# The time-mix scan: mask by block level taken from the solved products to the known triangular factor

## The reference

```
def step(S, inp):
    r_t, w_t, k_t, v_t, a_t, b_t = inp
    sa = jnp.einsum('bhij,bhj->bhi', S, a_t)
    S = S * w_t[:, :, None, :] + sa[..., None] * b_t[:, :, None, :] + v_t[..., None] * k_t[:, :, None, :]
    return S, jnp.einsum('bhij,bhj->bhi', S, r_t)
```

## Time and profile before

| | us |
|---|---|
| three runs: median (lowest to highest) | 1450.24 (1449.11 to 1451.15) |
| the profiled execution, its own time | 1440.16 |
| its span in the trace | 1438.4 |
| TensorE busy | 1405.0 (98%) |
| DVE busy | 926.4 (64%) |
| ACT busy | 326.8 (23%) |
| GpSimd busy | 26.6 (2%) |

### The profile page before, as it was taken

One profiled execution on the slowest core, in us unless ns is written; L12 is line 12 of the kernel. 1 busy time (PEld: TensorE's weight loads), 2 busy tenths in 40 slices (PEclk: granted clock), 3 DMA queues, 4 the chain that ended last, 5 costly groups with the idle time before them and its releaser, 6 DMA issues.

```text
span 1438.4 us, 30683 instructions
## 1 busy us (share of the span) xinstructions
PE 1405.0 (98%) x13056; PEld 1289.7 (90%) x13056; DVE 926.4 (64%) x1868; ACT 326.8 (23%) x660; POOL 26.6 (2%) x32
## 2 busy tenths in 40 slices
PE   9999999999999999999899999999999999999997
PEld 7899888999999977878887999999997779999997
DVE  3288433358866475868645787787684447878875
ACT  2134103240000131420121322221104632222211
POOL 0140000000001000000000000000000000000000
PEclk9999999999999999999999999999998999999999
DMA  9434344255445413420000444344442104444451
GB/s 371 160 137 158 121 161 146 102 155 207 163 174 177 147 59 118 147 89 5 4 4 16 149 159 157 137 158 178 179 161 89 59 31 147 161 141 168 152 191 69
DMA packets 56994, 190.75 MB, mean 133 GB/s; under 512 B 9216, under 2 KB 11392, under 8 KB 56608
## 3 DMA queue, kind: packets, MB, share of 16 engines
q1 hardware_dynamic: 50768, 180.93, 35.3%
q10 hardware_dynamic: 6096, 7.91, 1.7%
HBM read 187.77 MB, written 1.05 MB: 131 GB/s over the span
## 4 chain that ended last, share of the span: by engine, by line
PE 94%; DVE 3%; ACT 1%; issue 1%; DMA 0%; ACTq 0%; DVEq 0%; PEldq 0%
PE ps L1925 93%; DVE arena L1713 1%; DMA arena<-in_x_t 0%; PE ps L1180 0%; DVE rs L2410 0%; DVE arena L1740 0%; ACT arena L2358 0%; DVE arena L1664 0%; PE ps L2128 0%; PE ps L2019 0%; DVE arena L1741 0%; DVE arena L1619 0%; DVE arena L874 0%; DVE arena L876 0%; DVE arena L1724 0%
## 5 line engine op out<-in xcount | busy, mean ns | idle before, releaser
L1925 PE MATMUL ps<-arena,ring 128*128 128x128 f32 (+6 forms) x4720 | 801.3, 321 | 3.2 <-DMA ring<-in_stream 1.1
L1925 PEld LDWEIGHTS ps<-arena,ring 128*128 128x128 f32 x4720 | 705.0, 191 | 69.1 <-issue 7.7
L1925 PE MATMUL ps<-arena 64*64 64x64 f32 (+9 forms) x7110 | 588.0, 258 | 13.0 <-issue 6.1
L1925 PEld LDWEIGHTS ps<-arena 128*128 128x128 f32 (+4 forms) x7110 | 529.5, 163 | 43.6 <-issue 23.3
L874 DVE TENSOR_TENSOR arena<-ring 128x512 f32<-128x512 f32 x104 | 71.8, 690 | 119.4 <-PE ps L1925 85.6
L861 ACT COPY arena<-ps 128x128 f32<-128x128 f32 (+2 forms) x76 | 20.2, 266 | 353.8 <-PE ps L1925 353.8
L1690 DVE SCALAR_TENSOR_TENSOR arena<-arena,cols 128x271 f32<-128x271 f32 (+3 forms) x176 | 82.9, 492 | 9.8 <-ACT arena L1322 6.7
L1925 PE MATMUL ps<-arena,consts 128*128 128x260 f32 (+9 forms) x368 | 75.6, 348 | 7.3 <-DVE arena L1868 3.0
L1322 ACT ACTIVATE arena<-arena,cols 128x272 f32<-128x272 f32 (+1 forms) x88 | 48.8, 601 | 122.8 <-DVE arena L1619 68.9
L876 DVE TENSOR_TENSOR arena<-arena,ring 128x512 f32<-128x512 f32 x104 | 72.4, 696 | 3.6
L1925 PEld LDWEIGHTS ps<-arena,consts 128*128 128x128 f32 (+3 forms) x368 | 54.8, 183 | 21.8 <-issue 3.5
(11 more groups left out here) (283 smaller groups left out, 896.6 us busy)
## 6 DMA issues: line engine op xcount, KB each, us to landing
ring<-in_stream SPq DMA_DIRECT2D x342, 512.0 KB, 3.6
consts<-in_consts ACTq DMA_DIRECT2D x1, 1580.0 KB, 12.7
arena<-in_mem_t ACTq DMA_DIRECT2D x1, 1024.0 KB, 7.3
res<-in_x_t ACTq DMA_DIRECT2D x1, 1024.0 KB, 19.1
out_t<-arena SPq DMA_DIRECT2D x4, 256.0 KB, 2.5
arena<-in_x_t ACTq DMA_DIRECT2D x3, 256.0 KB, 5.5
arena<-in_g ACTq DMA_DIRECT2D x1, 640.0 KB, 6.4
arena<-in_w ACTq DMA_DIRECT2D x2, 256.0 KB, 4.9
```

The source lines that it names most:

```text
L1925: return nc.tensor.matmul(out, lhs, rhs, start=start, stop=stop)
```

## The change

The mask of a level keeps whole blocks of rows and columns, and `tm` is block-diagonal in blocks of that size, so masking the factor before the product gives the same as masking the product after it. The change does that:

- GpSimd, at the end of its program, makes 23 masked copies of `gram[c]`, one for each turn (c, m), each by two multiplications of 64 partitions x 512 (upper and lower half), ahead of TensorE's use. The copies lie in seven places that are free at that time: `tmt[2]`, `tmt[3]`, `tmt[4]`, later `tmt[0]`, then four quarters of `gram[0]`. A place is overwritten only when the `grow_y` that read it last is done.
- `grow_y` on TensorE takes the masked copy instead of `gram[c]`, and waits for it in each of the 23 turns.
- The product is masked already: ACT copies it from PSUM to `ysb`, and DVE's multiplication (L1734) goes away. ACT's list, a loop over the chunks before, is now written out with the 23 copies in it.
- The level constants are transposed, since the factor lies transposed in `gram`.

```diff
-        parts[f"level{m}"] = (h // (2 * m) == t // (2 * m)) & (h % (2 * m) >= m) & (t % (2 * m) < m)
+        parts[f"level{m}"] = (h // (2 * m) == t // (2 * m)) & (h % (2 * m) < m) & (t % (2 * m) >= m)
...
+        level_masked = sem("level_masked")
+        quarter = [arena[:, chunk_at + n * KT * CH:chunk_at + (n + 1) * KT * CH].rearrange("p (q j) -> p q j", q=KT)
+                   for n in range(4)]
+        LEVEL_TILE = (12, 13, 14, 12, 13, 14, 13, 14, 13, 14, 14, 10, 0, 1, 2, 3, 0, 1, 2, 3, 0, 1, 2)
+        at_level = [tmt[n - 10] if n >= 10 else quarter[n] for n in LEVEL_TILE]
+        GROWN = {0: (0, 2, 4), 1: (1, 3, 5, 6, 8), 2: (7, 9, 10, 12, 14), 3: (11, 13, 15, 16, 18), 4: (17, 19, 20, 21, 22)}
...
             def grow_y(c, m):
-                li = LEVELS.index(m)
+                li, n = LEVELS.index(m), turn_of(c, m)
+                pe.wait_ge(level_masked, 2 * n + 2)
                 pe.wait_ge(t_added[c % 2], added_before(c) + 2 * li + 1)
-                if li == 0:
-                    pe.wait_ge(gram_masked, 4 * c + 4)
                 for q, p in pairs:
                     r = HALF[p]
-                    last = mm(ps[HALF[1 - p], 2 * (c % 2) + 1, q * CH:(q + 1) * CH], gram[c][r, q, p, 0:CH],
+                    last = mm(ps[HALF[1 - p], 2 * (c % 2) + 1, q * CH:(q + 1) * CH], at_level[n][r, q, :],
                               tm[c % 2][r, q, :])
...
+            def grown(c, m):
+                li = LEVELS.index(m)
+                act.wait_ge(y_ready[c % 2], past(c, 0) + li + 1)
+                act.wait_ge(u_ready[c % 2], past(c, 1) + li + 1)
+                cp(ysb[c % 2], ps[:, 2 * (c % 2) + 1, :].rearrange("p (q j) -> p q j", q=KT)
+                   ).then_inc(y_masked[c % 2], 1)
...
-            for c in range(NC):
-                turn(c)
...
+            for m in LEVELS[:3]:
+                grown(0, m)
+                grown(1, m)
+            grown(1, 16)
+            turn(0)
+            grown(2, 2)
+            grown(1, 32)
+            keys(0)
...
+            turn(1)
+            grown(2, 16)
+            grown(3, 4)
+            keys(1)
...
-            def grow_y(c, m):
-                li = LEVELS.index(m)
-                dve.wait_ge(y_ready[c % 2], past(c, 0) + li + 1)
-                dve.wait_ge(u_ready[c % 2], past(c, 1) + li + 1)
-                tt(ysb[c % 2], blocks(2 * (c % 2) + 1), over(const(f"level{m}"), KT), ALU.mult).then_inc(y_masked[c % 2], 1)
...
+            def masked(c, m):
+                n = turn_of(c, m)
+                pool.wait_ge(gram_masked, 4 * c + 4)
+                same = [k for k in range(n) if LEVEL_TILE[k] == LEVEL_TILE[n]]
+                if same:
+                    d, li = [(d, turns.index(same[-1])) for d, turns in GROWN.items() if same[-1] in turns][0]
+                    pool.wait_ge(y_ready[d % 2], past(d, 0) + li + 1)
+                elif n == 11:
+                    pool.wait_ge(uu_ready, 1)
+                elif n >= 12:
+                    pool.wait_ge(o_ready, 1)
+                for p in range(2):
+                    r = HALF[p]
+                    g.tensor_tensor(at_level[n][r], gram[c][r, :, p, 0:CH], const(f"level{m}")[r, :].unsqueeze(1).to_broadcast([CH, KT, CH]),
+                                    ALU.mult).then_inc(level_masked, 1)
+            pool.wait_ge(ev["lora"], GB + 24)
+            masked(0, 2)
+            masked(1, 2)
+            masked(0, 4)
+            masked(1, 4)
+            masked(0, 8)
+            masked(1, 8)
+            masked(1, 16)
+            masked(2, 2)
+            masked(1, 32)
+            masked(2, 4)
+            masked(2, 8)
+            masked(3, 2)
...
```

More of the change, by code:

```diff
@@ L581, in program, with turn_of @@
         u_ready, t_added = [sem(f"inv_u{i}") for i in range(2)], [sem(f"inv_added{i}") for i in range(2)]
+        level_masked = sem("level_masked")
[4 more added lines that the diff above has]
+        GROWN = {0: (0, 2, 4), 1: (1, 3, 5, 6, 8), 2: (7, 9, 10, 12, 14), 3: (11, 13, 15, 16, 18), 4: (17, 19, 20, 21, 22)}
+        def turn_of(c, m):
+            return GROWN[c][LEVELS.index(m)]
         def past(c, more):
@@ L1375, in root @@
                 f(s16a[0:16, part], s16a[0:16, part], ACT.Sqrt).then_inc(y_act.sem, 1)
-            f(small[0:16, 60:61], small[0:16, 0:1], ACT.Sqrt)
-            for c in range(NC):
-                turn(c)
[L1379 to L1389, removed]
+            def grown(c, m):
[4 more added lines that the diff above has]
+                   ).then_inc(y_masked[c % 2], 1)
+            f(small[0:16, 60:61], small[0:16, 0:1], ACT.Sqrt)
+            for m in LEVELS[:3]:
[6 more added lines that the diff above has]
+            keys(0)
+            grown(2, 4)
+            upper(0)
+            grown(2, 8)
+            grown(3, 2)
+            answer(0)
+            turn(1)
+            grown(2, 16)
+            grown(3, 4)
+            keys(1)
+            grown(2, 32)
+            grown(3, 8)
+            upper(1)
+            answer(1)
+            grown(3, 16)
+            turn(2)
+            grown(4, 2)
+            grown(3, 32)
+            keys(2)
+            grown(4, 4)
+            upper(2)
+            grown(4, 8)
+            answer(2)
+            turn(3)
+            grown(4, 16)
+            keys(3)
+            upper(3)
+            grown(4, 32)
+            answer(3)
+            turn(4)
+            squared_a(0)
+            squared_a(1)
+            keys(4)
+            squared_a(2)
+            squared_a(3)
+            upper(4)
+            root("a", PART_A)
+            answer(4)
             y_pe.wait(act, "centred_b")
@@ L1768, in chunk_vector @@
             for m in LEVELS[:3]:
-                grow_y(0, m)
-                grow_y(1, m)
                 grams(LEVELS.index(m) + 2)
@@ L1774, in chunk_vector @@
             slope(2)
-            grow_y(1, 16)
             flip(2)
             grow_u(1, 16)
-            grow_y(2, 2)
-            grow_y(1, 32)
             grow_u(2, 2)
@@ L1782, in chunk_vector @@
             slope(3)
-            grow_y(2, 4)
             lower(0)
@@ L1786, in chunk_vector @@
             grow_u(2, 4)
-            grow_y(2, 8)
-            grow_y(3, 2)
             gain(0)
@@ L1791, in chunk_vector @@
             grow_u(3, 2)
-            grow_y(2, 16)
-            grow_y(3, 4)
             recall(1)
@@ L1796, in chunk_vector @@
             grow_u(3, 4)
-            grow_y(2, 32)
-            grow_y(3, 8)
             lower(1)
@@ L1803, in chunk_vector @@
             gain(1)
-            grow_y(3, 16)
             flip(4)
             grow_u(3, 16)
-            grow_y(4, 2)
-            grow_y(3, 32)
             recall(2)
@@ L1811, in chunk_vector @@
             grow_u(3, 32)
-            grow_y(4, 4)
             lower(2)
             grow_u(4, 4)
-            grow_y(4, 8)
             gain(2)
             grow_u(4, 8)
-            grow_y(4, 16)
             recall(3)
@@ L1821, in chunk_vector @@
             lower(3)
-            grow_y(4, 32)
             gain(3)
@@ L2734, in _ @@
                     pool2.reach(ins, "wa_scaled")
+            def masked(c, m):
[26 more added lines that the diff above has]
+            masked(3, 2)
+            masked(2, 16)
+            masked(3, 4)
+            masked(2, 32)
+            masked(3, 8)
+            masked(3, 16)
+            masked(4, 2)
+            masked(3, 32)
+            masked(4, 4)
+            masked(4, 8)
+            masked(4, 16)
+            masked(4, 32)
 def blocks_of(w):
```

## The result

The changed kernel takes 1451.13 us (median of 20 runs, 1447.3 to 1457.72); the kernel before, run beside it, 1447.93 us (20 runs, 1440.37 to 1452.77). The medians lie 3.2 us apart. The ratio on record, which is not that of the two medians, is 1.0034, 95% from 1.002 to 1.0047: 0.0034 x 1447.93 = 4.9 us slower. A second set, on the same chip as the kernel before again, gave 1.0062 (1.0041 to 1.0083), 9.0 us. So the change makes the kernel slower, by 0.3% in one set and 0.6% in the other, where 0.2% can be told from no change. The time is in the range given; the case that came nearest is rival 1, and one cost was in no case.

The account below looks back on a forecast made before the run. TensorE, paced by its instruction fetches (3.45 us per block of 256), was taken as the bound, so DVE's relief gains 0. Costs 1.74 + 0.5 + 0.24 = 2.5 us on 1450.24 give 1452.7 us, range 1449.2 to 1455.8.

Parts of the forecast that it names:

- rival 1: At `grow_y(3, 2)`: GpSimd is late again if a pair takes over 2.3 us; 5.0 us slower, 1455.2 us; chance 0.13.
- What bounds the kernel: TensorE in the scan waits for its own instructions, no block of 256 under 3.45 us; taking the mask from DVE gains 0.
- The copy on ACT: 23 copies of 0.589 us, 13.5 us on a little-used ACT, covered by TensorE's work between `grow_y` and `grow_u`: cost nothing.
- The extra wait: A second wait instruction on TensorE in 18 of 23 `grow_y` turns: 0.24 us if all fall into paced blocks.
- Where the cost is: Before `grow_y(1, 2)`, GpSimd's copy now stands between causal masks and TensorE: delay 1.74 us (1.2 to 2.3).
- from there to the end all is shifted by the same amount: Sign that the forecast is right: after TensorE's added idle before `grow_y(1, 2)`, everything later moves by one equal delay.
- Rival 3: The delay at 653 us is absorbed if instruction fetches run ahead: 1.6 of 2.5 us given back, 1451.1 us; chance 0.15.
- GpSimd and DVE at once: GpSimd's first copies meet DVE adds L1724 of chunks 0 and 1, lengthening DVE's chain by 0.5 us (0 to 1.7).
- The pair of GpSimd: Two 64 x 512 multiplications before `grow_y(1, 2)`: 1.6 us, the middle of 1.04 (both at once) and 2.16 (in turn).
- rival 4: GpSimd's two halves run side by side, 1.04 us a pair: 1.9 us slower, 1452.2 us; chance 0.2.
- The sum: Delay at `grow_y(1, 2)` 1.74, slowed adds 0.5 and extra waits 0.24: 2.5 us slower (1.2 to 4.2), 1452.7 us.

Follow-up runs that it names:

- second profiles of before and of after: Nothing changed: the kernel before and the changed kernel each run and profiled once more; ratios to the kernel before 1.0005 and 1.0062.
- third profile of before: Nothing changed: the kernel before run and profiled a third time; ratio 1.0009, levels time 113.84 us.
- kept-busy run: Changed kernel plus four unread 128 x 512 products on TensorE ahead of `grow_y(1, 2)`; ratio 1.0024 to the kernel before.

## Why the prediction was right and wrong

**What bounds the kernel: right.** DVE's relief is worth nothing (mask left out: 1.0006), and "issue" is TensorE's largest wait in every profile. That it stands for the fetch of instructions is read from the spacing of the blocks and the fetched packets; no run changed the stream of instructions to show it. And 3.45 us is not the least for a block: the second profiles of before and of after each have one of 256 instructions in 3.35 (731.62 to 734.97 and 736.20 to 739.56). The 10.00 of 10 us of DVE in the earlier trace rows are true and mean nothing for the end.

**The copy on ACT: right**, 585 ns each, and in no wait of TensorE.

**The extra wait, 0.24 us:** the instructions are there, as TensorE has 379 wait instructions in the trace of after and 361 in that of before, 18 more. What they cost is too small to be told from the rest; neither shown nor refuted.

**Where the cost is: right for the larger part.** It is before `grow_y(1, 2)`, behind an idle time of GpSimd that ends with the causal mask, and it isn't won back: from `grow_y(3, 2)` to the last `grow_u` it took 66.3 and 67.1 us after, 65.5 and 66.1 in the second and third profile of before (63.8 in the shown one). Two turns done the old way take most of the cost out. Rival 3 falls. But "from there to the end all is shifted by the same amount" did not hold: the delay is 3.6 us at `grow_y(1, 2)`, 4.9 at `grow_y(0, 4)`, and 6.5 and 8.3 at `grow_y(3, 2)`.

**GpSimd and DVE at once: right, at twice the size.** 0.5 us was taken (0 to 1.7); 0.9 to 1.0 is what it costs. Both adds were put too low. The first was to be 0.4 late and was 0.65: the sum took 1.04 us for GpSimd's instruction, and with its 1.27 the same working, 647.62 + 1.27 + 0.55 = 649.44, gives the measured end, 649.45. The second was put at 0.1 and was 0.36 late, as the second half of the pair ran behind the first and was still there when it began (until 647.62 + 2.96 = 650.58, against 650.08). The rule quoted from the Trainium skill (SBUF — State Buffer, "Who interferes with whom") is borne out by the traces: the add with two inputs in SBUF took 1.34 and 1.05 us, the mask with one input in PSUM between them 0.68.

**The pair of GpSimd: wrong; this term was mis-sized.** "From below, both halves at once: 1.04. From above, one behind the other: 1.12 + 1.04 = 2.16 ... so I take the middle, 1.6". It is 2.6 us, above the upper end. Both halves of the reasoning failed. The halves don't run side by side (1.34 us from start to start), so rival 4 falls, and what the Trainium skill says in the GPSIMD Engine Reference ("Instruction dispatch") isn't seen here as an overlap of instructions on different partitions. And a copy of 64 partitions isn't at most as long as one of 128: it takes 1.27 us against 1.04 in the earlier trace rows. Why is not shown. The second input is a broadcast in both, but there one value stands for 64 elements in a row, and here a mask of 64 x 64 is repeated for eight heads. The upper bound was therefore none: it took a row of another shape and operand pattern for a ceiling.

**The second wait, rival 1: it happened**, at the place named, and past the point named: "It decides from 2.3 us a pair". Two pairs took 5.62 us; 1.2 us of wait were worked out from 2.9 a pair; 0.6 of idle time came, 0.8 by the starts of the two turns. The time that it gave, 5.0 us more, is close to the 4.9 measured in the comparison of the change, and 4.0 under the 9.0 of the second. It had a chance of 0.13, since the size of the pair had been put under 2.3.

**The clock: in no case.** TensorE's wait grew from 0.52 to 4.07 us, and the prediction counted only the time of that wait. The half clock behind it costs 1.7 us up to `grow_u(0, 2)` and 1.3 up to `grow_y(0, 4)`, by the kept-busy run; whether more than nothing of it is left at the end is not shown.

**The sum.** Adds 1.0, pair 2.6 and clock 1.3 are 4.9 us at `grow_y(0, 4)`, which starts at 19.05 and 19.06 in the two executions of after and at 14.12 in all three of before. With 0.8 for the second wait it is 5.7 us, where 2.5 was predicted (with 0.24 for the waits). The typical levels times differ by 8.5. The 2.8 left over are not attributed: after has blocks of instructions 3.98 us apart (669.10 to 673.08) where before had 3.45 to 3.61, the second profile of after 3.5 to 4.0, and one execution of each kernel can't tell a cause from chance, as the three levels times of before, 2.2 us apart, show. The ratios, which have many runs, lie at 4.9 and 9.0, on both sides of the named 5.7.

Against the median of three runs from which the forecast started, 1450.24, this is 1451.13; the 20 runs beside it put before at 1447.93. So the time came near the forecast of 1452.7 partly by luck, as the starting median was high; the difference is the better test, and it was twice the forecast in the first set and more in the second.

No version here is faster than the kernel before. The best of the changed ones leave the two first turns on DVE, 1.0012 and 1.001, and can't be told from it.

## What to carry to other kernels

An engine that is busy for a whole stretch need not bound it: ask which wait ends last on the engine that does, and run the kernel once with the work left out (1.0006 here), which bounds what moving it can give. Work moved to an idle engine ahead of time is free only where there is time ahead; at the first use after a start-up the full latency of the new engine stands on the path, so do the first uses the old way (here that took 6.9 us off the median, on the same chip). And a bound taken from a row with another shape or operand pattern isn't a bound: leave room above it, and ask what TensorE's clock does if the wait comes out several us long.

## What the runs showed of the hardware

- GpSimd multiplies 64 x 512 fp32 in 1.27 us, and in 1.61 us beside a DVE add with two inputs in SBUF; two such on opposite halves of the partitions take some 2.6 us together.
- After TensorE had been idle for 4.07 us (3.17 in one kernel), the granted clock was half for some 3.4 us, and the steps up to `grow_u(0, 2)` took 1.7 us longer. With 1.40 and 1.60 us idle at the same place the clock stayed up, as it did with unread products in the wait. Elsewhere in the scan it fell for 3.4 us behind waits of 0.74, 1.01 and 1.79 us, in one profile each.
- The clock also halved for 10 to 17 us, starting between 772 and 784 us, in 10 of the 14 profiles, with the change or without it, with TensorE busy 8.5 to 10 of the 10 us before; it was in neither profile of the first comparison.
- TensorE's blocks of 256 short instructions came 3.35 to 3.45 us apart at the closest (3.45 from 664.46 to 667.91 in the shown profile of before, 3.35 from 731.62 to 734.97 in the second); 669.10 to 673.08, 3.98 us, in the profile of after is one of the slower ones.
